# Last down products ahead of a combination, two pairs' bias loaded ahead, output weights ahead of the last two modulation chunks

## The chip, the cores and the metric

The kernel runs on one core of one Trainium2 chip. The metric is the device time of one execution, in microseconds (us); lower is better. TensorE (PE) multiplies into PSUM, VectorE (DVE), ScalarE (ACT) and GpSimd (POOL) work on SBUF and PSUM, and SyncE (SP) issues nearly all DMA transfers, in the order in which its program lists them. An engine runs its instructions in program order and waits on semaphores where another engine's result is needed.

## The reference

256 tokens of width 1024 pass through two blocks of two layers each. Every layer is a mixer followed by a mixture of experts (MoE), all in float32. The change touches the MoE of all four layers and the mixers of the second block.

```python
for i in range(DEPTH):                      # second block, DEPTH = 2
    mod = (silu(c) @ w_ada[i] + b_ada[i]).reshape(b, 6, d)        # modulation: 6 vectors of 1024
    hm = rmsnorm(x, norm_mix[i]) * (1 + sc_m) + sh_m
    y = dilated_mixer(hm, ...) if i == 0 else forgetting_mixer(hm, ...)   # ends with  o @ w_out
    x = x + g_m * y
    hf = rmsnorm(x, norm_ffn[i]) * (1 + sc_f) + sh_f
    x = x + g_f * hierarchical_moe_2(hf, ...)                     # top-1 group, top-2 experts of 16

# dilated mixer, for each of 16 head slots and three dilation groups:
logits = einsum(q, k) + bias            # bias from a table, by distance and head
p = softmax(logits); out = p @ v        # the groups' outputs merged by their softmax denominators

# mixture of experts
hid = silu(t @ w_gate[e]) * (t @ w_up[e])
y = sum over e of (hid * gate[e]) @ w_down[e]
```

The first block's two MoE have 32 experts, the second block's 16.

## The kernel before

**The weight ring.** All large weights pass through one buffer of 24576 columns in SBUF (`ring`). The class `Stream` (lines 49 to 96) fixes at build time the list of chunks in the order of the list, the place of each in the ring, and how many earlier chunks must have been given back (`chunk_used`) before a chunk may be loaded (`need`). `issue` walks that list in order on SP's queue: a chunk whose place isn't free yet holds back all behind it. A chunk is 4096 columns (2 MB) for 512 columns of a projection, 6144 columns (3 MB) for a modulation chunk (768 of w_ada's columns), 2048 columns (1 MB) for a third of an expert: pieces 0 and 1 hold gate and up for the lower and the upper half of k, piece 2 holds down.

**Modulation chunks.** 16 chunks of w_ada are slipped in among other weights by `weight_amid`. DVE turns one into partial sums by `ada_part` (lines 402 to 409, eight operations), then PE sums over the partitions by `ada_sums` (36 products of one column for three chunks), and DVE copies the result and finishes it (`after`).

**Output projection of the second block's mixers**, `project_rows` (line 426), called for `a_w_out_2` and `b_w_out_2` with `ada=[1, 2]`. Two weight chunks c = 0, 1, each with two units (one for each half of the tokens), eight K steps of 512 columns each. The chunks stand in the ring as modulation 1, weights 0, modulation 2, modulation 3, weights 1. DVE: copy of the gate row to `grow`, modulation chunk 1, units 0 and 1 (two operations each, in `add_rows`: times gate, plus x), modulation chunks 2 and 3, then units 2 and 3. A modulation chunk is given back when DVE has finished it, a weight chunk when DVE reaches its second unit (`free_chunk`). By the places in the ring, weights 1 lie where modulation chunk 1 lies, so that they can be loaded only when DVE has given that one back.

**Dilated attention**, `dilated_attention` (line 1103), twice (two halves of the heads), four pairs i of heads each. The bias of a pair is six DMAs of 128 KB (2 heads times 3 groups, `bias_load`, line 2757), which gather rows of a table in HBM. Pair 0's are issued before the half's projection ends, behind a wait until the last q and k rows have been turned (`load_last` in `project_heads_split`). Pair 1's are the first thing SP issues in the attention. Pair 2's wait until pair 0's logits are made, pair 3's until pair 1's are. DVE adds bias to scores and takes the maximum (L1216), ACT takes the exponential (L1255), DVE scales (L1224), PE transposes (L1175), ACT copies (L1263), PE multiplies by the values (L1185), in the order written out in `dilated_attention`.

**Experts**, `moe` (line 1294). For expert e PE runs, in this order: `gate_up(e + 1, 0)` (L1528), `turn(e)` (L1539, a transposition of the hidden rows), `combine(e - 1)` (L1561), `gate_up(e + 1, 1)`, `down(e)` (L1550). DVE: `hidden(e)` (L1771), `low(e - 1)` (L1791), `take_turned(e)` (L1775), `slots(e + 1)`. ACT: silu (L1653), then `high(e - 1)` (L1644). `down(e)` needs take_turned(e); `high(e)` needs down(e), `low(e)` needs high(e), `combine(e)` needs low(e). In the last expert the two gate_up are absent.

## Time and profile before

| | |
|---|---|
| three runs | 1701.11, 1706.50, 1706.56 us (median 1706.5) |
| profiled execution | 1701.91 us, span 1700.2 us, 1.7 us around the span |
| PE / PE weight load busy | 1559.8 us (92%) / 984.6 us (58%) |
| DVE / ACT / POOL busy | 809.8 us (48%) / 506.4 us (30%) / 135.8 us (8%) |
| mean granted TensorE clock | 0.963 |
| DMA | 467.27 MB, mean 275 GB/s |

A share of busy time says which engine is used most, not what a stage waits for. For each stage the time line and the waits tell what came last. The granted clock is the share of TensorE's full 2.4 GHz; it stands at 1.00 or at 0.50 (1.2 GHz), and a figure between the two is a stretch in which it changed. In a row of the time line "[0.36 <-PE PS L1539]" means that the engine was idle for 0.36 us before the instruction, until PE's L1539 released it. Rows with a count xN merge N instructions; the second number is then their common stretch.

The stages that the change touches, by their first and last instructions in the time line: the four MoE end at about 441, 875, 1384 and 1692 us; the dilated attention runs at 995.7 to 1040.9 and 1155.6 to 1200.3 us; the output projections at 1200.6 to 1240.2 and 1508.0 to 1547.6 us.

### The profile page before, as it was taken

The page shows a single profiled execution, that of the slowest core. Times are in us where ns is not written, and L with a number is a line of the kernel's source. Part 1 is how long each engine was busy: PE and PEld are TensorE (multiplying, and loading weights), DVE is VectorE, ACT ScalarE, POOL GpSimd, SP SyncE. Part 2 cuts the span into 40 slices and gives each one's busy share as a digit, 9 for nine tenths or more (in the row PEclk, how much of TensorE's full clock was granted, in tenths as well). Part 3 has the DMA queues.
Part 4 walks back from the last instruction along what each step waited for, and adds up shares of the span by engine and source line. Part 5 has one row for each costly group of instructions (what it writes and reads, how often), then busy time and mean ns, then how long its engine had stood idle before and what let it go on. Part 6 is the DMA issues. An engine that isn't in the chain of part 4 may idle for free. (4 is left out here: it accounts for less than half of the span.)

```text
span 1700.2 us, 23212 instructions
## 1 busy us (share of the span) xinstructions
PE 1559.8 (92%) x8906; PEld 984.6 (58%) x8906; DVE 809.8 (48%) x1863; ACT 506.4 (30%) x1015; POOL 135.8 (8%) x158
## 2 busy tenths in 40 slices
PE   8999899998799999999979988997889969889997
PEld 4585555554375555555447766775475547646553
DVE  1755533332335444333346645664663346576333
ACT  3230211111126212111135645555131135631211
POOL 0000211000000021001010001000021010002110
PEclk9999999999899989999999989999989989998999
DMA  8977289999761366999995351244449973626794
GB/s 365 371 285 282 90 357 420 421 421 420 314 277 75 126 249 247 420 421 420 421 398 222 137 211 51 100 180 166 177 173 400 421 320 124 248 92 257 300 421 196
DMA packets 62109, 467.27 MB, mean 275 GB/s; under 512 B 7664, under 2 KB 15776, under 8 KB 17184
## 3 DMA queue, kind: packets, MB, share of 16 engines
q1 hardware_dynamic: 61984, 465.59, 67.5%
q8 instruction: 79, 1.29, 0.3%
q14 instruction: 46, 0.38, 0.1%
HBM read 462.81 MB, written 2.76 MB: 274 GB/s over the span
## 5 line engine op out<-in xcount | busy, mean ns | idle before, releaser
L1528 PE MATMUL PS<-ring,catT 128*64 128x256 f32 x3072 | 368.5, 383 | 16.2 <-DMA ring<-in_moe 8.9
L1528 PEld LDWEIGHTS PS<-ring,catT 128*64 128x64 f32 x3072 | 213.6, 137 | 186.9 <-issue 82.1
L783 PE MATMUL PS<-w_split,h_split 128*128 128x512 f32 x1152 | 276.2, 398 | 10.4 <-DVE w_split L868 10.4
L783 PEld LDWEIGHTS PS<-w_split,h_split 128*128 128x128 f32 x1152 | 214.8, 190 | 65.3 <-DVE w_split L868 17.1
L1550 PE MATMUL PS<-ring,hidden_cols 128*64 128x512 f32 x768 | 183.1, 598 | 0.0
L868 DVE TENSOR_TENSOR w_split<-ring,w_split 128x512 fp32r<-128x512 f32 x192 | 131.9, 708 | 77.0 <-ACT w_split L816 76.6
L1791 DVE SCALAR_TENSOR_TENSOR xn_split<-PS,slot_w,xn_split 128x512 fp32r<-128x512 f32 x96 | 72.1, 751 | 192.1 <-ACT xn_split L1644 192.1
L816 ACT CAST w_split<-ring 128x512 fp32r<-128x512 f32 x192 | 118.2, 620 | 114.2 <-PE PS L783 113.7
L1653 ACT ACTIVATE hidden_rows<-PS 128x128 f32<-128x128 f32 x96 | 26.6, 277 | 412.8 <-PE PS L1528 412.8
L1561 PE MATMUL PS<-xn_split,back 64*128 64x512 f32 x768 | 114.4, 416 | 13.6 <-DVE xn_split L1791 13.5
L1644 ACT ACTIVATE xn_split<-PS,slot_w 128x512 fp32r<-128x512 f32 x96 | 66.0, 687 | 156.7 <-PE PS L1550 156.7
L1412 POOL COPY catT<-xsT 128x576 f32 x96 | 64.1, 668 | 584.2 <-PE PS L1528 517.3
L476 PE MATMUL PS<-ring,catT 128*128 128x512 f32 x224 | 100.3, 609 | 8.3 <-DMA ring<-in_b_w_out 3.7
L1771 DVE TENSOR_TENSOR hidden_rows<-PS,hidden_rows 128x128 f32<-128x128 f32 x96 | 28.0, 292 | 157.2 <-ACT hidden_rows L1653 157.2
L407 DVE SCALAR_TENSOR_TENSOR ada_part<-ring,silu_c,ada_part 128x768 f32<-128x768 f32 x98 | 99.9, 1019 | 3.4
L1550 PEld LDWEIGHTS PS<-ring,hidden_cols 128*64 128x64 f32 x768 | 53.9, 137 | 71.5 <-issue 56.9
L1561 PEld LDWEIGHTS PS<-xn_split,back 64*128 64x128 f32 x768 | 65.5, 184 | 36.7 <-issue 18.8
L476 PEld LDWEIGHTS PS<-ring,catT 128*128 128x128 f32 x224 | 43.5, 196 | 63.1 <-issue 54.2
L1396 POOL TENSOR_SCALAR xsT<-x,stat 128x1024 f32<-128x1024 f32 x8 | 22.8, 2846 | 684.3 <-DVE stat L1702 684.0
L1783 DVE SCALAR_TENSOR_TENSOR back<-catT,picked 128x256 fp32r<-128x256 f32 x96 | 46.5, 485 | 57.1 <-PE PS L1561 56.8
L1618 ACT ACTIVATE xn_split<-x 128x1024 fp32r<-128x1024 f32 x8 | 8.5, 1058 | 170.2 <-PEq L447 119.9
L1775 DVE COPY hidden_cols<-PS 128x128 f32<-128x128 f32 x96 | 28.0, 292 | 48.9 <-PE PS L1539 48.7
(417 smaller groups left out, 1811.5 us busy)
## 6 DMA issues: line engine op xcount, KB each, us to landing
ring<-in_moe SPq DMA_DIRECT2D x288, 1024.0 KB, 14.6
ring<-in_w_ada SPq DMA_DIRECT2D x16, 3072.0 KB, 14.0
ring<-in_a_w_in SPq DMA_DIRECT2D x23, 2048.0 KB, 10.0
ring<-in_b_w_in SPq DMA_DIRECT2D x8, 2048.0 KB, 17.8
ring<-in_a_w_out SPq DMA_DIRECT2D x2, 3072.0 KB, 10.3
ring<-in_b_w_out SPq DMA_DIRECT2D x2, 3072.0 KB, 10.4
ring<-in_w_mem_kv SPq DMA_DIRECT2D x2, 2048.0 KB, 12.1
ring<-in_a_w_out SPq DMA_DIRECT2D x2, 2048.0 KB, 8.3
```

The source lines that it names most:

```text
L407: dlink(nc.vector.scalar_tensor_tensor(part, w[:, k, :], silu_c[:, k:k + 1], part, ALU.mult, ALU.add))
L476: last = nc.tensor.matmul(PS[:, i % 8, 0:n], srcT[:, j, t * P:(t + 1) * P], w[:, j, o:o + n], start=j == 0, stop=j == k - 1)
L783: last = nc.tensor.matmul(PS[:, 2 * (i % 2) + t, :], hs[:, hp, k, t * P:(t + 1) * P], wk[:, (KT * i + k) % splits, wp, :], start=k == 0 an ...
L816: nc.scalar.copy(wk[:, (KT * i + k) % splits, 0, :], w[:, k, :]).then_inc(w_high.sem, 1)
L868: nc.vector.tensor_tensor(wk[:, (KT * i + k) % splits, 1, :], w[:, k, :], wk[:, (KT * i + k) % splits, 0, :].bitcast(F32), ALU.subtract).t ...
L1412: nc.gpsimd.tensor_copy(xf[:, e % 2], xsT[:, :, bass.ds(start, WIN)]).then_inc(win_ready.sem, 1)
L1528: last = nc.tensor.matmul(PS[half * WIN:(half + 1) * WIN, 4 + e % 2, 0:2 * P].rearrange("p (g f) -> p g f", g=2), xf[:, e % 2, k, :], gate ...
L1550: last = nc.tensor.matmul(PS[c * WIN:(c + 1) * WIN, 6 + e % 2, :], hs[:, e % 2, f2, :], wd[:, f2, c * BANK:(c + 1) * BANK], start=f2 == 0, ...
L1561: last = nc.tensor.matmul(PS[:, 2 * t + c, :], back[c * WIN:(c + 1) * WIN, e % 2, t * P:(t + 1) * P], yk(e % 2, h)[c * WIN:(c + 1) * WIN], ...
L1644: nc.scalar.activation(yk(e % 2, 0), PS[:, 6 + e % 2, :], ACT.Copy, scale=slot_w[:, e % 2, :]).then_inc(y_high.sem, 1)
L1783: nc.vector.scalar_tensor_tensor(back[:, e % 2, :], ranks[:, 1, :], slot_of[:, e:e + 1], picked[:], ALU.is_equal, ALU.add).then_inc(back_r ...
L1791: nc.vector.scalar_tensor_tensor(yk(e % 2, 1), PS[:, 6 + e % 2, :], slot_w[:, e % 2, :], yk(e % 2, 0).bitcast(F32), ALU.mult, ALU.subtract ...
```

## The change

Three edits.

1. In the last expert, PE does `down(E - 1)` ahead of `combine(E - 2)`, and DVE does `take_turned(E - 1)` ahead of `low(E - 2)`. All other experts stay as they were.
2. Pair 1's bias is issued together with pair 0's, in `load_last`. It goes to `grow` and to columns 5 to 7 of `catT`, instead of `grow` and a tile of its own; pair 3 still uses `grow` and that tile. SP's program in the attention begins with pair 2.
3. In the two output projections the ring's order becomes modulation 1, weights 0, weights 1, modulation 2, modulation 3. DVE does modulation chunks 1 and 2 ahead of units 0 and 1, and chunk 3 ahead of units 2 and 3. Modulation chunks 2 and 3 are given back together, behind unit 3.

```diff
-        c_aout2 = weight_amid("a_w_out_2", 8, [512] * 2, [1, 2])
+        c_aout2 = weight_amid("a_w_out_2", 8, [512] * 2, [1, 0], 2)
-        c_bout2 = weight_amid("b_w_out_2", 8, [512] * 2, [1, 2])
+        c_bout2 = weight_amid("b_w_out_2", 8, [512] * 2, [1, 0], 2)
@@ project_rows
-                    stream.issue(nc, sp, first + len(widths) + sum(ada))
+                    stream.issue(nc, sp, first + len(widths) + n_ada)
@@ project_rows, vector
                             for _ in range(ada[c]):
                                 ada_part(dve, ada0 + done, part[:, done, :])
                                 done += 1
-                            if ada[c] and done == sum(ada):
+                            if ada_last:
+                                ada_part(dve, ada0 + done, part[:, done, :], False)
+                                done += 1
+                            if done == n_ada:
                                 nc.vector.sem_inc(part_ready.sem, 1)
...
+                    for _ in range(ada_last):
+                        nc.vector.sem_inc(chunk_used, 1)
@@ dilated_attention, sync
-                    for i in range(1, n):
-                        if i >= 2:
-
-                            sp.wait_ge(*logits_ready[1].at(2 * (i - 1)))
+                    for i in range(2, n):
+                        sp.wait_ge(*logits_ready[1].at(2 * (i - 1)))
                         for y in range(2):
-                            bias_load(2 * i + y, bias[i % 2][y], bias_loaded[i % 2].sem)
+                            bias_load(2 * i + y, bias[i][y], bias_loaded[i % 2].sem)
@@ moe, tensor
                             turn(e)
-                            if e:
+                            if e + 1 < E:
+                                if e:
+                                    combine(e - 1)
+                                gate_up(e + 1, 1)
+                                down(e)
+                            else:
+                                down(e)
                                 combine(e - 1)
-                            if e + 1 < E:
-                                gate_up(e + 1, 1)
-                            down(e)
@@ moe, vector
                             hidden(e)
-                            if e:
+                            if e + 1 == E:
+                                take_turned(e)
                                 low(e - 1)
-                            take_turned(e)
+                            else:
+                                if e:
+                                    low(e - 1)
+                                take_turned(e)
@@ dilated mixer
-                        bias = [[first_bias[:, 0], first_bias[:, 1]]]
+                        other_bias = grow[:, 0:3 * T].rearrange("p (s k) -> p s k", s=3)
+                        bias = [(first_bias[:, 0], first_bias[:, 1]), (other_bias, catT[:, 5:8, :])]
-                        def load_first_bias(sp):
-                            for y in range(2):
-                                bias_load(y, bias[0][y], sig("bias_loaded0").sem)
+                        def load_two_biases(sp):
+                            for i in range(2):
+                                for y in range(2):
+                                    bias_load(2 * i + y, bias[i][y], sig(f"bias_loaded{i}").sem)
-                        bias.append([grow[:, 0:3 * T].rearrange("p (s k) -> p s k", s=3), sbuf(s2, "bias", [P, 3, T])[:]])
+                        bias += [bias[0], (other_bias, sbuf(s2, "bias", [P, 3, T])[:])]
-            project_rows(catT, 8, c_aout2, [512] * 2, add_rows(grow[:]), ada=[1, 2], after=...)
+            project_rows(catT, 8, c_aout2, [512] * 2, add_rows(grow[:]), ada=[1, 0], ada_last=2, after=...)
```

## Rows read from the trace of the kernel before

**Rows 1.** Waits of the whole span: us in total, times, longest.
```profile
PE PS L1561 <- DVE xn_split L1791: 13.5, 8, 1.8
DVE logits L1216 <- DMA bias<-bias_dram: 7.2, 2, 4.5
PE PS L476 <- DMA ring<-in_b_w_out: 3.7, 1, 3.7
PE PS L476 <- DMA ring<-in_a_w_out: 3.6, 1, 3.6
```

**Rows 2.** Time line, end of the fourth MoE: start us, us, engine, line.
```profile
1678.84 0.33 PE L1539 MATMUL PS<-ident,hidden_rows 128*128 128x128 f32 x1
...
1679.20 0.29 DVE L1775 COPY hidden_cols<-PS 128x128 f32<-128x128 f32 x1 [0.36 <-PE PS L1539]
...
1683.81 0.33 PE L1539 MATMUL PS<-ident,hidden_rows 128*128 128x128 f32 x1
...
1685.69 1.20 PE L1561 MATMUL PS<-xn_split,back 64*128 64x512 f32 x8 [1.55 <-DVE xn_split L1791]
...
1686.82 1.94 PE L1550 MATMUL PS<-ring,hidden_cols 128*64 128x512 f32 x8
```

**Rows 3.** Time line, end of the first MoE, the last down products.
```profile
434.75 3.62 PE L1550 MATMUL PS<-ring,hidden_cols 128*64 128x512 f32 x8
```

**Rows 4.** Table by stretches: us, busy by engine, granted clock, DMA share, GB/s.
```profile
436.00:438.00 2.00, 2.00 (x6) 0.24 (x2) 0.00 (x0) 0.00 (x0) 0.00 (x0) 0.50 0.98 418
...
1166.00:1168.00 2.00, 0.00 (x0) 0.00 (x0) 1.96 (x7) 1.30 (x4) 0.00 (x0) 0.50 0.55 189
...
1181.00:1182.00 1.00, 1.00 (x7) 0.67 (x4) 0.42 (x2) 1.00 (x3) 0.00 (x0) 1.00 0.06 22
```

**Rows 5.** Time line, first output projection of the second block.
```profile
1202.52 13.90 PE L476 MATMUL PS<-ring,catT 128*128 128x512 f32 x32
...
1203.98 0.62 DVE L405 TENSOR_SCALAR ada_part<-ring,silu_c 128x768 f32<-128x768 f32 x1
...
1212.06 0.33 SPq L93 DMA_DIRECT2D ring<-in_a_w_out  x1
1212.12 0.70 DVE L1289 TENSOR_TENSOR PS<-PS,grow 128x512 f32<-128x512 f32 x1
...
1212.86 0.69 DVE L1290 TENSOR_TENSOR x<-x,PS 128x512 f32<-128x512 f32 x1
...
1220.00 15.64 PE L476 MATMUL PS<-ring,catT 128*128 128x512 f32 x32 [3.58 <-DMA ring<-in_a_w_out]
...
1235.47 4.08 PE L423 MATMUL PS<-ones_f,ada_part 128*128 128x1 f32 x36
```

**Rows 6.** DMA issues at 1115 to 1117 us: KB each, us to landing.
```profile
ring<-in_w_ada SPq DMA_DIRECT2D x1, 3072.0 KB, 10.0
```

**Rows 7.** Time line, dilated attention of the first half.
```profile
1006.60 1.54 PE L1175 MATMUL PS<-ident,logits 128*128 128x128 f32 x6 [4.75 <-DVE logits L1224]
...
1014.03 2.01 PE L1185 MATMUL PS<-probsT,dv 128*64 128x128 f32 x24
```

**Rows 8.** Time line, dilated attention of the second half.
```profile
1165.92 0.56 DVE L1216 CUSTOM_DVE_ANT_1 logits<-PS,grow 128x384 f32<-128x384 f32 x1 [4.52 <-DMA bias<-bias_dram]
...
1168.29 1.54 PE L1175 MATMUL PS<-ident,logits 128*128 128x128 f32 x6 [6.57 <-DVE logits L1224]
...
1174.05 1.48 PE L1185 MATMUL PS<-probsT,dv 128*64 128x128 f32 x24
...
1174.45 1.81 SPq L2757 DMA_DIRECT2D grow<-bias_dram  x3
...
1178.92 0.88 PE L1175 MATMUL PS<-ident,logits 128*128 128x128 f32 x6 [0.66 <-DVE logits L1224]
...
1182.92 1.48 PE L1185 MATMUL PS<-probsT,dv 128*64 128x128 f32 x24
```

**Rows 9.** Time line, the third MoE's first expert products.
```profile
1273.51 5.40 PE L1528 MATMUL PS<-ring,catT 128*64 128x256 f32 x48 [1.87 <-POOL catT L1412]
```

More of the change, by code:

```diff
@@ L170, in build, with weight_amid @@
         ada_at = []
-        def weight_amid(name, k, widths, ada):
+        def weight_amid(name, k, widths, ada, ada_last=0):
             first = len(stream.chunks)
-            for ap, n in zip(chunk_aps(A[name], k, widths), ada):
+            for ap, n in zip(chunk_aps(A[name], k, widths) + [None], ada + [ada_last]):
                 for _ in range(n):
@@ L178, in weight_amid @@
                     stream.add([ada_aps[len(ada_at) - 1]])
-                stream.add([ap])
+                if ap is not None:
+                    stream.add([ap])
             return first
@@ L424, in ada_sums, with project_rows @@
             return last
-        def project_rows(srcT, k, first, widths, evac, cut=BANK, ada=None, after=None, aside=None, router=None, gate=None):
+        def project_rows(srcT, k, first, widths, evac, cut=BANK, ada=None, after=None, aside=None, router=None, gate=None, ada_last=0):
             ctx_rows = ExitStack()
@@ L433, in project_rows @@
             ada0 = sum(at < first for at in ada_at)
-            part = sbuf(ctx_rows, "ada_part", [P, sum(ada), 768]) if sum(ada) else None
+            n_ada = sum(ada) + ada_last
+            part = sbuf(ctx_rows, "ada_part", [P, n_ada, 768]) if n_ada else None
             part_ready, ada_made = sig("ada_part_ready"), sig("ada_made")
@@ L482, in _ @@
                             pe.wait_ge(*rows_taken.at(len(units)))
-                        ada_sums(sum(ada), part).then_inc(ada_made.sem, 1)
+                        ada_sums(n_ada, part).then_inc(ada_made.sem, 1)
                 def free_chunk(eng, i):
@@ L1214, in add_bias @@
                     def add_bias(i, t, y):
-                        nc.vector.tensor_tensor_reduce(logits(i, t, y), score(t, y), bias[i % 2][y][:, :, T - (t + 1) * P:T],
+                        nc.vector.tensor_tensor_reduce(logits(i, t, y), score(t, y), bias[i][y][:, :, T - (t + 1) * P:T],
                                                        1.0, 3.0e38, ALU.add, ALU.min, mx[:, i % 2, t, 0, y:y + 1]).then_inc(logits_ready[t].sem, 1)
@@ L2757, in bias_load @@
                                 nc.sync.dma_start(dst[:, g, :], src).then_inc(loaded, 16)
-                        def load_first_bias(sp):
-                            for y in range(2):
-                                bias_load(y, bias[0][y], sig("bias_loaded0").sem)
-                        project_heads_split(hT, c_ain2 + half * 9, jobs, rows=z_rows, load_last=load_first_bias,
+                        def load_two_biases(sp):
+                            for i in range(2):
+                                for y in range(2):
+                                    bias_load(2 * i + y, bias[i][y], sig(f"bias_loaded{i}").sem)
+                        project_heads_split(hT, c_ain2 + half * 9, jobs, rows=z_rows, load_last=load_two_biases,
                                             norm=(mod_gain[:, 0, 0, :], mod[:, 0, 0:8]) if half == 0 else None)
-                        bias.append([grow[:, 0:3 * T].rearrange("p (s k) -> p s k", s=3), sbuf(s2, "bias", [P, 3, T])[:]])
+                        bias += [bias[0], (other_bias, sbuf(s2, "bias", [P, 3, T])[:])]
                         def head(h):
@@ L2771, in build @@
                         dilated_attention([head(h) for h in range(8)], bias, bias_load)
-            project_rows(catT, 8, c_aout2, [512] * 2, add_rows(grow[:]), ada=[1, 2], after=lambda: modulation(1, (0, 24), (0,)), router=2, gate=mod[:, 0, 16:24])
+            project_rows(catT, 8, c_aout2, [512] * 2, add_rows(grow[:]), ada=[1, 0], ada_last=2, after=lambda: modulation(1, (0, 24), (0,)), router=2, gate=mod[:, 0, 16:24])
         if stop >= 7:
@@ L2843, in build @@
                 attention([head(h) for h in range(16)], True, key_bias, key_loaded)
-            project_rows(catT, 8, c_bout2, [512] * 2, add_rows(grow[:]), ada=[1, 2], after=lambda: modulation(1, (24, 48), (1,)), router=3, gate=mod[:, 1, 16:24])
+            project_rows(catT, 8, c_bout2, [512] * 2, add_rows(grow[:]), ada=[1, 0], ada_last=2, after=lambda: modulation(1, (24, 48), (1,)), router=3, gate=mod[:, 1, 16:24])
         if stop >= 9:
```

## The prediction

> **What bounds the kernel now.** I read the waits of the whole span first, because the shares of busy time say little here: PE is busy 92% of the span, so a gain must be a place where PE stands still, or runs at half clock, and nothing else covers it. Three kinds of such places answer to the three edits [rows 1]: PE waits for DVE ahead of a combination, 8 times and 13.5 us in all, two in each MoE's end; DVE waits for a bias load, twice, 7.2 us; PE waits for output weights, twice, 3.6 and 3.7 us. Then the time line around each place, to see what comes next if the wait goes. Last the granted clock there: it stands at 0.50 in the stretch behind each of the longer standstills [rows 4], so a removed wait can give back more than its own length.
>
> **Edit 1, the ends of the four MoE.** At the fourth, the last transposition starts at 1683.81, PE then waits 1.55 us for DVE's `low(14)`, combines at 1685.69 and starts the last down products at 1686.82 [rows 2]. In an ordinary expert DVE's copy of the transposed tile starts 0.36 us behind the transposition (1678.84, 1679.20) and takes 0.29 [rows 2]. With the copy first, it runs at 1684.17 to 1684.46, and down starts some 0.15 later, at 1684.6: 2.2 us earlier. DVE's `low(14)` isn't delayed: it ended just ahead of the combination at 1685.69, so it began about 1684.8, behind the copy. The moved combination (1.2 us) then runs between 1686.5 and 1687.7, while ACT and DVE turn the down products into `high` and `low`, in which time PE had nothing; the last combination only has to follow `low(15)`. All that comes later hangs on this chain, so 2.2 us come off. Bounds: 0 if the combination cost on the path what the reordering gives, 3.2 if both of PE's waits (1.55 and 1.8) went but for two latencies; I take 2.2. The other three ends have the same order. Four times 2.2 is **8.8 us**. The first MoE has a surplus: its last down products took 3.62 us instead of 1.94 [rows 2, 3], at a granted clock of 0.50 [rows 4]. Started 2.2 us earlier, at 432.6, they would be over by 434.5, ahead of where they now start; I count the difference, **1.7 us**, with 0 as the other bound. No wait is added: `low(E-2)` waits for ACT as before, and the copy ahead of it needs only the transposition.
>
> **Edit 2, the bias of pair 1.** Second half: DVE waited 4.52 us, until 1165.92 [rows 8]. Without the DMA, next is the scores of pair 1: PE had finished them when it went idle, at 1168.29 - 6.57 = 1161.72 [rows 8]. So DVE starts at about 1161.8, 4.1 us earlier, and PE's transposition follows it by 1168.29 - 1165.92 = 2.37 us, at 1164.2. First half: PE idle since 1006.60 - 4.75 = 1001.85, so its transposition can start at 1001.85 + 0.1 + 2.37 = 1004.3 instead of 1006.6 [rows 7]: 2.3 us. That is 6.4 us of plain waiting.
>
> Behind the wait comes the clock. From this transposition to the end of the value products the second half took 1174.05 + 1.48 - 1168.29 = 7.24 us, the first 1014.03 + 2.01 - 1006.60 = 9.44, and a later pair at full clock 1182.92 + 1.48 - 1178.92 = 5.48 [rows 7, 8]. The clock was 0.50 at 1166 to 1168 [rows 4]. If it stays up this gives back 1.8 and 4.0 us, 5.8 in all. The two bounds are 0 and 5.8. PE would still be idle for about 2.4 us, against 0.66 in a later pair [rows 8] and at most 1.8 in the MoE's ends [rows 1], of which the fourth kept the clock (1.94 us for down [rows 2]). I take 5.8. Sum of the edit: **12.2 us**.
>
> The six moved DMAs cost SP 3.7 us of issue (1.81 for three [rows 8], twice) in the projection, and what is behind them in the queue comes 3.7 us later: in the first half weights for the second half, in the second half the output weights and modulation chunks, wanted 50 us on. I cost that at nothing; it costs at most those 3.7 us if that cover is gone. Pair 2's bias still waits for pair 0's logits. It would be issued from about 1161.4; a quiet load of six went out at 1174.45 and its traffic ended by 1181 to 1182 [rows 4, 8], 7 us at most, so it lands by 1168.5. Pair 2 wants it about 1 us behind pair 0's values, 1169.6 + 1 = 1170.6. The slack is 2 us; in the first half 1001.5 + 7 = 1008.5 against 1010.8.
>
> **Edit 3, the output projections.** Now weights 1 are issued when modulation chunk 1 is given back (1212.06) and PE stands from 1216.42 to 1220.00; its second half then takes 15.64 us instead of 13.90 [rows 5]. With weights 1 early PE would be done at 1216.42 + 13.90 = 1230.3. Now DVE is the bound: three chunks of 8.05 us (1203.98 to 1212.06, less a little) and two units of 1.46 (0.70 and 0.69 with gaps) from 1203.98 make 1203.98 + 24.2 + 2.9 = 1231.1 [rows 5]. The 36 small products start at 1231.3 instead of 1235.47: **4.2 us**. What follows them is unchanged. Chunk 3 takes the wait that weights 1 had: issued at 1212.06, a 3 MB load on a quiet queue lands 10.0 us later [rows 6], 1222.1, and DVE wants it at 1223.0. It is hidden by 0.9 us. At best 5.3 us, if DVE had no part in it (3.58 and 1.74); the other way, each us that the load takes beyond 10.9 takes one off, and at 15.1 nothing is left. The other projection repeats the pattern [rows 1]. Twice 4.2 is **8.4 us**.
>
> The give-back moves: weights 0 from about 1216.5 to 1221.5, and the rest of the ring behind unit 3, at 1234. Ten of the next MoE's first twelve pieces (1 MB each) go out at 1232 to 1234. At 418 GB/s [rows 4] ten take 25 us, until 1259; PE wants the first at 1273.51 - 4.2 = 1269.3 [rows 9]. Hidden, by 10 us.
>
> One rule weighs on the clock term. PE's new idle stretch in the attention is a wait for DVE; at the first MoE's end PE had only waited for DVE (1.55 us and more) and was at 0.50 at 436 to 438 [rows 4]. The Trainium skill ("TensorE: Matmul & The Clock Gate", section "Loop structure matters more than you think") says that a DVE copy between groups of products leaves the array warm and that a wait for a DMA is what cools it. By it the 5.8 us are sure; by the row they are not, which is rival 1.
>
> **Sum.** 8.8 + 1.7 + 12.2 + 8.4 = 31.1 us. The profiled execution took 1701.91, so 1670.8. It lies at the lower of two levels of the runs (1701.1; 1706.5 twice), the median 4.6 above it. I know no term that says which level the changed kernel will take, and put the forecast in the middle: 1670.8 + 2.3 = **1673 us**.
>
> **Rivals.**
> 1. *The clock stays low.* PE is idle in the attention for 2.4 us and the small transpositions after it may run at 0.50 all the same, and so may the first MoE's last down. Against it: the later pairs and the fourth MoE's end kept it. Then 5.8 + 1.7 are missing: 1678.3 on the lower level, 1683 on the upper.
> 2. *The next load is late.* Chunk 3 lands 3 us later than I say, and pair 2's bias 1 us behind its need: twice 2.1 and twice 1, with 2 us of clock each time, 10 us: 1683. For it: slacks of 0.9 and 2 us. Against it: both queues are quiet then.
> 3. *The edits don't do what they say.* The bias still comes from behind something on SP's queue, or the moved combination lands on the path again (1.2 us of the 2.2 in each MoE, 4.8), and the attention gives nothing: 1701.9 - 31.1 + 12.2 + 4.8 + 2.3 = 1690.
> 4. *Slower: the experts' first weights come late.* Place: the third and the fourth MoE, since ten pieces are now issued only at 1232 to 1234. Price: each us by which they land behind 1269.3. It decides when both stand for over 15.5 us (31.1 in all), when ten pieces take over 51 us, a rate under 206 GB/s. While bias rows were gathered the rate was 189 GB/s [rows 4]; at it they take 55.5 us, landing at 1289, 20 us late, twice 40 us: 1702 + 9 = 1711. Against it: pieces of the ring moved at 418 [rows 4].
>
> **How the numbers follow.** Forecast 0.66, rival 1 0.19, rival 2 0.06, rival 3 0.03, slower 0.02, and 0.04 for a time below 1666 (more clock given back in the routers). The range takes in both levels and rivals 1 and 2: 1670.8 less 4 for terms that reach their better bound, 1667, to 1684. What measurement can tell from no change is about 0.3%, 5 us: faster 0.96, same 0.02, slower 0.02.
>
> **What would show it.** Right: no idle time of DVE before L1216 for a bias DMA, PE's transposition about 2.4 us after it fell idle, clock 1.00 there; L476 as one run of 64 products in 27.8 us, then under 1 us before the small products; DVE's L1775 ahead of L1791 at the MoE's ends, with 2.4 us from the transposition's end to PE's next combination. Wrong: a clock of 0.50 behind either attention's first pair; a wait of DVE for w_ada or of L1216 for z_rows; any wait of L1528 for the ring at the third MoE's start.

## The result and the profile after

The changed kernel took 1689.0 us (median of four runs, 1676.21 to 1689.67), the kernel before, run beside it, 1706.5; the ratio is 0.9881, with a 95% interval of 0.9836 to 0.9927. Six more runs of it later gave 1688.4 (1678.60 to 1692.52; 0.989, 0.9854 to 0.9927). So it is faster by 1.2%, about 19 us, where 31 us and 1673 were forecast. The profiled execution took 1689.67 us, with a span of 1687.9 and a mean granted clock of 0.955, against 1701.91, 1700.2 and 0.963 before.

Every wait that the prediction set out to remove is gone or as small as forecast. What comes behind them isn't as forecast: the granted clock, and two waits of PE that grew.

The waits of the whole span, after (engine, line waited for, us in total, times, longest). They answer to [rows 1]: 8 waits of 13.5 us ahead of a combination are 4 of 2.7 us, and there is no row of L1221 (L1216 before) waiting for a bias DMA, nor of L478 (L476 before) waiting for the ring.

```profile
PE PS L1566 <- DVE xn_split L1799: 2.7, 4, 0.7
PE PS L424 <- DVEq L525: 1.6, 2, 0.8
```

The time line at the end of the fourth MoE, PE alone (start us, us). It answers to [rows 2].

```profile
1673.69 0.33 PE L1544 MATMUL PS<-ident,hidden_rows 128*128 128x128 f32 x1
1674.45 1.94 PE L1555 MATMUL PS<-ring,hidden_cols 128*64 128x512 f32 x8 [0.43 <-issue]
1676.32 1.20 PE L1566 MATMUL PS<-xn_split,back 64*128 64x512 f32 x8
1678.20 1.20 PE L1566 MATMUL PS<-xn_split,back 64*128 64x512 f32 x8 [0.67 <-DVE xn_split L1799]
```

From the last transposition to the last down products it is 0.76 us (forecast: 0.79), and the moved combination stands in a time in which PE had nothing.

The time line of the second half's attention, DVE's first operation on pair 1 and PE behind it. It answers to [rows 8].

```profile
1150.53 0.55 DVE L1221 CUSTOM_DVE_ANT_1 logits<-PS,grow 128x384 f32<-128x384 f32 x1
...
1153.16 1.54 PE L1180 MATMUL PS<-ident,logits 128*128 128x128 f32 x6 [2.24 <-DVE logits L1229]
1154.63 1.23 PE L1147 MATMUL PS<-dkT,dqT 64*128 64x256 f32 x4
1155.79 1.54 PE L1180 MATMUL PS<-ident,logits 128*128 128x128 f32 x6
```

DVE has no idle time ahead of it, and PE waits 2.24 us (forecast: 2.4). But both transpositions take 1.54 us, the time of half clock, where a later pair takes 0.88 [rows 8]. The table by stretches says the same (us, busy by engine with the number of instructions, granted clock, DMA share, GB/s):

```profile
1153.00:1157.00 4.00, 3.84 (x16) 2.79 (x16) 1.99 (x6) 1.90 (x6) 0.00 (x0) 0.50 0.49 167
```

The time line of the first output projection and the start of the router behind it, PE alone. It answers to [rows 5].

```profile
1190.33 27.63 PE L478 MATMUL PS<-ring,catT 128*128 128x512 f32 x64
1218.75 5.62 PE L424 MATMUL PS<-ones_f,ada_part 128*128 128x1 f32 x36 [0.79 <-DVEq L525]
1226.25 3.64 PE L1436 MATMUL PS<-ident,x 128*128 128x128 f32 x16 [1.89 <-PEq L449]
1229.69 3.44 PE L1442 MATMUL PS<-catT,mod 128*128 128x20 f32 x16
1232.96 6.99 PE L1448 MATMUL PS<-catT,hT 128*128 128x20 f32 x32
```

The projection is one run of 64 products, as forecast. Then the small products take 5.62 us instead of 4.08 [rows 5], since the clock falls 2.4 us behind their start, PE stands for 1.89 us, and the router's products run at half clock. The kernel before, in the same place:

```profile
1240.49 3.55 PE L1431 MATMUL PS<-ident,x 128*128 128x128 f32 x16 [0.94 <-PEq L447]
1243.87 1.86 PE L1437 MATMUL PS<-catT,mod 128*128 128x20 f32 x16
1245.58 5.50 PE L1443 MATMUL PS<-catT,hT 128*128 128x20 f32 x32
```

The stretch of after, by the table by stretches: PE is busy for 14.75 of 15 us, and the clock doesn't come back.

```profile
1226.00:1241.00 15.00, 14.75 (x70) 14.79 (x71) 3.90 (x11) 4.69 (x7) 9.94 (x4) 0.50 1.01 421
```

The wait of 1.89 us (0.94 before) ends just behind SP's last issue of the experts' weights, most of which edit 3 holds back until unit 3. SP's row in the same stretch is over at 1225.81, 0.44 us ahead of PE's 1226.25:

```profile
1219.58 6.23 SPq L93 DMA_DIRECT2D ring<-in_moe  x10
```

Behind the third MoE, PE's first transpositions of the next mixer wait for PE's own sequencer, and longer than before. Before, after, and in the kernel with zeros in the attention and around the small products (f_both, described below):

```profile
1394.04 3.58 PE L769 MATMUL PS<-ident,catT 128*128 128x128 f32 x16 [9.59 <-PEq L1301]
1384.50 3.65 PE L776 MATMUL PS<-ident,catT 128*128 128x128 f32 x16 [12.22 <-PEq L1306]
1371.02 3.65 PE L780 MATMUL PS<-ident,catT 128*128 128x128 f32 x16 [8.73 <-PEq L1313]
```

### The profile page after: what moved, and what is told of

The parts are those of the page before. It is cut to its first block and busy times, and to the rows that moved or that the text cites. A ratio compares the mean times of both kernels' runs of the same rounds, so it can differ in the third digit from the quotient of the medians.

```text
span 1687.9 us, 23214 instructions
## 1 busy us (share of the span) xinstructions
PE 1569.2 (93%) x8906; PEld 994.5 (59%) x8906; DVE 807.0 (48%) x1863; ACT 506.3 (30%) x1015; POOL 136.4 (8%) x158
## 5 line engine op out<-in xcount | busy, mean ns | idle before, releaser
L478 PE MATMUL PS<-ring,catT 128*128 128x512 f32 x224 | 96.7, 592 | 1.1 <-PEq L982 1.1
L478 PEld LDWEIGHTS PS<-ring,catT 128*128 128x128 f32 x224 | 42.3, 190 | 53.3 <-issue 53.3
## 6 DMA issues: line engine op xcount, KB each, us to landing
ring<-in_moe SPq DMA_DIRECT2D x288, 1024.0 KB, 14.9
ring<-in_w_ada SPq DMA_DIRECT2D x16, 3072.0 KB, 12.2
ring<-in_b_w_in SPq DMA_DIRECT2D x8, 2048.0 KB, 17.6
ring<-in_b_w_out SPq DMA_DIRECT2D x2, 3072.0 KB, 10.5
```

The lines of the kernel that those rows point to most:

```text
L478: last = nc.tensor.matmul(PS[:, i % 8, 0:n], srcT[:, j, t * P:(t + 1) * P], w[:, j, o:o + n], start=j == 0, stop=j == k - 1)
```

## The experiments

Two things were open. First, whether each edit is worth what was forecast, alone and beside the others. Second, whether the lowered clock is what took the rest, and what lowers it. Unless a line says otherwise a time is the median; "alone" is the kernel before with one edit. All were timed against the kernel before on the same chip, and ratios come with their 95% intervals. In the profile rows, tiles named `PS<-zero` are products of zeros; `keep_busy(bank, n)` issues n of them, 512 columns each. The kernel before has some of its own, in the routers.

### Each edit alone

The edits are those of the diff above, one at a time; the extracts below only name them.

**Edit 1 alone.**

```diff
 moe: last expert
-combine(e - 1); down(e)        low(e - 1); take_turned(e)
+down(e); combine(e - 1)        take_turned(e); low(e - 1)
```

> The kernel before with edit 1 alone (the order in the last expert of each MoE). Theory (the waits went as forecast, TensorE's clock took part of it back): the four ends give 8.8 us and the first MoE's last down nothing more, since the clock falls just behind it: about 6 to 9 us off. Rival (the prediction's terms hold, each edit by itself): 8.8 + 1.7 = 10.5 us off.

Measured: 1699.16 us (12 runs), ratio 0.9954 (0.9934 to 0.9975), 7.2 us under the kernel before. The theory, though the interval (4.3 to 11.3 us) holds the rival's 10.5 too.

**Edit 2 alone.**

```diff
-load_last=load_first_bias
+load_last=load_two_biases
```

> The kernel before with edit 2 alone (pair 1's bias loaded with pair 0's). Theory: both waits for a bias DMA are gone, 6.4 to 8 us, but the granted clock is 0.50 behind the first pair as before, for 7 to 10 us, so that the transposition that took 1.54 us still takes 1.54: 5 to 8 us off in all. Rival: the clock stays at 1.00 there, the transposition takes 0.88 us, 12.2 us off.

Measured: 1693.48 us (8 runs), ratio 0.9936 (0.9905 to 0.9967), 12.9 us by the medians. By this run alone it is the rival. Its profile shows the waits gone, and a granted clock that did fall in the attention: in the first half the transposition took 1.54 us again (in the second half 0.88, and the one behind it 1.54).

```profile
1001.71 1.54 PE L1173 MATMUL PS<-ident,logits 128*128 128x128 f32 x6 [2.24 <-DVE logits L1222]
1003.18 1.23 PE L1140 MATMUL PS<-dkT,dqT 64*128 64x256 f32 x4
```

**Edit 3 alone.**

```diff
-ada=[1, 2]
+ada=[1, 0], ada_last=2
```

> The kernel before with edit 3 alone (the order of weights and modulation chunks in the two output projections). Theory: the projection is one run of 64 products in some 27.7 us and the small products start 4 us sooner, but they and the router behind them then stand at a granted clock of 0.50 for 20 us or more where it was 10, which costs 4 to 5 us each: between 1 us faster and 3 us slower in all. Rival: 8.4 us off, the clock has no part in it.

Measured: 1698.32 us (12 runs), ratio 0.9958 (0.9937 to 0.9980), 8.0 us by the medians. Neither theory's loss nor a proof of the rival: the router behind the first projection took 1.7 us more than before, and PE's wait for SP at its start was 2.60 us instead of 0.94, which is nearly all of it; the other router lost nothing.

**The changed kernel again.**

> The changed kernel again, to see how far its times lie apart. Theory: the time follows the share of the span at half clock, so that runs with a mean granted clock near 0.967 are near 1676 us and those near 0.956 near 1689 us, and nothing lies below the line through them. Rival: the two levels have to do with the DMA, and the mean clock of a run says nothing about its time.

Measured: 1688.43 us (6 runs). The time does follow the clock: the run at 1678.60 has a mean granted clock of 0.964, that at 1692.52 has 0.953. But the line isn't sharp, and it isn't a matter of this kernel: the 68 runs of the kernel before that were made beside the experiments lie anywhere from 1694.0 to 1713.8 us (median 1705.5, mean 1704.9), its mean clock from 0.954 to 0.964. Five runs at 0.963 or more have a mean of 1698.7 us, thirteen at 0.956 or less one of 1708.7.

By their medians the three edits alone add up to 28 us, and together they gained 18. With such a scatter that can be chance, so kernels with one edit left out were run as well.

### One edit left out

```diff
 no_rows:  edits 1 and 2      no_bias:  edits 1 and 3      no_tails:  edits 2 and 3
```

> The changed kernel without edit 3 (edits 1 and 2 alone). By the single edits' medians, 7.2 and 12.9 us off, it stands at 1686 us. Theory (edit 3's wait is gone in the changed kernel, but its routers run at half clock and give it all back): 1684 to 1689 us, no slower than the changed kernel's 1688.7. Rival (edit 3 is worth its 4.2 us for each projection in the changed kernel too, and what is missing is missing elsewhere): 1695 to 1697 us.

Measured: 1689.76 us (6 runs), ratio 0.9916 (0.9892 to 0.9940).

> The changed kernel without edit 2 (edits 1 and 3). By the single edits, 7.2 and 8.0 us off: 1691 us. Theory (edit 2 is worth its two waits, 6.4 to 8 us, and no clock): 1695 to 1697 us. Rival (edit 2 is worth 12 us as forecast): 1701 us.

Measured: 1695.22 us (12 runs), ratio 0.9940 (0.9921 to 0.9960).

> The changed kernel without edit 1 (edits 2 and 3). By the single edits, 12.9 and 8.0 us off: 1685 us. Theory (edit 1 is worth 7 to 9 us on its own chain, at each MoE's end): 1696 to 1698 us. Rival (what is missing in the changed kernel is missing at the MoE's ends): 1688 to 1691 us.

Measured: 1691.18 us (12 runs), ratio 0.9935 (0.9913 to 0.9958).

Without edit 3 the time is 0.8 us above its theory's range, without edit 2 it is in its theory's (1695 to 1697), without edit 1 it is at its rival's (1688 to 1691). With intervals 7 to 8 us wide none decides by itself. Taken together they do. I fitted one time to each edit over all 140 runs of the kernels that hold any mix of the three (68 of before, 72 of the others), which assumes that the edits add up:

| edit | forecast | measured by the fit | measured in the segments below |
|---|---|---|---|
| 1, MoE ends | 10.5 | 5.7 ± 0.8 | 6.8 |
| 2, bias | 12.2 | 8.7 ± 0.8 | 8.7 |
| 3, output projections | 8.4 | 4.3 ± 0.8 | 4.0 |
| sum | 31.1 | 18.8 ± 1.0 | 19.5 |

(± is one standard error.) The fit meets the mean of each of the eight mixes within 1 us. Terms for pairs of edits, put into it, come out at 0.1 to 1.5 ± 1.7 us: no sign that one edit eats another, though 3 us of it couldn't be told. The 28 us of the single edits can be scatter; by means they are 25.

The third column is a second way to the same numbers, from the traces. The same DVE instruction is looked up in nine profiles (before, the changed kernel twice, and the six mixes), and the time between two such instructions is compared, kernels with the edit against kernels without it (means in us, with the least and the greatest, and behind them the mean us at a granted clock of 0.50 in the segment):

| segment | without | with | difference |
|---|---|---|---|
| first MoE's end, to 30 us behind it | 38.9 (37.6 to 40.4), 10.2 | 37.0 (35.9 to 37.4), 12.3 | -1.9 |
| second | 43.6 (43.3 to 43.8), 8.5 | 42.0 (41.2 to 42.5), 9.5 | -1.6 |
| third, to the next projection | 135.3 (134.8 to 135.6), 19.6 | 134.1 (133.1 to 134.9), 19.8 | -1.2 |
| fourth, to the kernel's end | 17.6 (17.4 to 17.8), 6.4 | 15.4 (15.3 to 15.4), 6.3 | -2.2 |
| attention, first half, start to pair 0's output | 19.6 (19.2 to 20.1), 11.1 | 16.8 (15.9 to 17.2), 9.5 | -2.8 |
| second half | 21.1 (18.8 to 22.1), 12.0 | 15.2 (14.2 to 17.4), 5.4 | -5.9 |
| output projection 1, to the small products' copy | 38.1 (36.7 to 39.5), 6.2 | 34.0 (33.9 to 34.1), 3.5 | -4.1 |
| router behind it, to the first expert | 38.1 (38.0 to 38.1), 10.8 | 41.1 (39.8 to 43.3), 18.4 | +3.1 |
| output projection 2 | 38.3 (36.8 to 39.6), 6.3 | 34.0 (32.4 to 35.0), 2.8 | -4.4 |
| router behind it | 38.0 (37.7 to 38.1), 10.7 | 39.4 (38.0 to 43.2), 14.9 | +1.4 |

The fourth MoE's end, where the time at 0.50 is the same with and without the edit, gives its 2.2 us within 0.4 in every kernel. Most of the scatter is in segments where the time at 0.50 scatters too: the same code of the second attention took 18.82 us with 6.8 us at 0.50 in the kernel before, and 21.99 with 13.7 in the kernel with edit 1 alone.

Three parts of these segments aren't the clock, and the table hides them:

- From the last expert's `hidden` to DVE's first operation on the residual rows it is 9.28 us without edit 1 and 7.03 with it, at all four ends and in all nine profiles but for one value: 10.97 at the first end of the kernel before. So edit 1's chain gives its 2.25 us at every end.
- Behind the third MoE, PE stood for 9.6 to 10.3 us without edit 1 and 11.8 to 12.7 with it, and the trace names PE's own sequencer. The other engines' rows of the same line of the program stand 1.0 to 1.7 us ahead of PE's start without edit 1 and 3.2 to 4.1 us with it. From the last `hidden` to the mixer's first DVE operation on `hT` the means are 23.9 us without and 23.8 with: nothing is left of edit 1 there, and the 1.2 us in the table come from further on. In the seven kernels with zeros below that have none at the MoE's ends this wait is 8.7 us, also where the zeros stand far from it. What holds PE's sequencer isn't shown.
- At the first router's start PE waited 0.94 us without edit 3 and 1.30 to 2.63 with it, a mean of 2.05; at the second's 1.63 in the changed kernel and 0.94 in the other eight profiles (0.30 where zeros stand ahead of it). In all nine routers of all kernels, with zeros or without, in which this wait was longer than usual, PE began 0.44 or 0.45 us behind the end of SP's last issue of expert weights; in the others SP had been done earlier. So 1.2 of the 4.5 us that the routers lost are SP's issues. That is read from the distance; no run issues them at another time.

### Holding the clock up

If a pause or light work of PE lowers the clock, products of zeros in its place must hold it. They write a part of PSUM that nobody reads.

**Zeros in the attention**, in the changed kernel:

```diff
                         if j == 2:
+                            if i == 0:
+                                for _ in range(18):
+                                    nc.tensor.matmul(PS[:, 3, 2 * P:4 * P], zero[:, 0:P], zero[:, 0:2 * P], ...)
                             pe.wait_ge(*probs_ready[1].at(i + 1))
```

> The changed kernel plus 18 products of zeros (256 columns, bf16, results never read) where PE waits 2.24 us for DVE ahead of the third transposition of pair 0, in both attentions. Theory (PE's pause there is what lowers the clock, and the lowered clock is what ate edit 2's second term): the stretch from the attention's start to pair 0's output falls from 14.2 to 17.4 us to about 14 us in both halves, no 0.50 there, some 5 us off in all against the changed kernel. Rival (the clock falls for what PE did before the pause, or the stretch is bound by DVE and ACT): the pause is filled, the stretch keeps its 16 to 17 us and its slow clock, no change.

Measured: 1672.98 us (5 runs), ratio 0.9817 (0.9794 to 0.9839), 15 us under the changed kernel, three times the theory's 5. The time line of PE and then the table by stretches, first half:

```profile
997.52 2.14 PE L1178 MATMUL PS<-zero 128*128 128x256 bf16 x18
999.83 0.87 PE L1183 MATMUL PS<-ident,logits 128*128 128x128 f32 x6 [0.17 <-DVE logits L1232]
```

```profile
998.00:1002.00 4.00, 3.83 (x32) 2.82 (x29) 3.11 (x9) 3.34 (x11) 0.00 (x0) 1.00 0.41 117
```

The clock is 1.00, the transposition takes 0.87 us, and from the attention's start to pair 0's output it is 12.7 us in both halves, against 17.0 and 17.4. That is 9.0 us. The rest isn't in the attention: between the two profiles 3.0 us more are gone in the first projection with its router, 4.2 behind the third MoE and 4.3 in the second projection with its router, in code that this edit doesn't touch. Of the 4.2, 3.5 are PE's wait for its own sequencer (8.72 us instead of 12.22), not the clock. How much of the rest the edit brings about, and how much is where the clock happened to stand in either profile, is left open.

**Zeros around the small products**:

```diff
+                        keep_busy(5, 3)
                         pe.wait_ge(*part_ready.at(1))
                         ada_sums(n_ada, part).then_inc(ada_made.sem, 1)
+                        keep_busy(5, 4)
```

> The changed kernel plus products of zeros around the 36 small products of both output projections, three (512 columns, bf16) ahead of them, where PE waits 0.8 us, and four behind them, where it waits 1.3 to 1.9 us. Theory one (the idle time around the small products starts the slow stretch): the stretch from the projection's end to the router's gather returns from 24.4 us to 21 us, 3 us off for each. Theory two (the small products of one column themselves count as little work): the clock still falls in them, nothing gained, up to 0.5 us lost each.

Measured: 1677.58 us (5 runs), ratio 0.9833 (0.9808 to 0.9859). Theory one's stretch: 20.3 and 20.2 us from the projection's output to the gather, instead of 24.6 and 24.4. In both the clock still fell in the small products, which took 5.6 and 5.7 us, as theory two had it, but it was back soon after the zeros. The time is 11 us under the changed kernel; the routers give 6.0 of them against the mean of the kernels with edit 3, and PE's wait behind the third MoE 3.5 against the profile of the changed kernel.

```profile
1219.16 5.62 PE L424 MATMUL PS<-ones_f,ada_part 128*128 128x1 f32 x36
1224.65 1.87 PE L354 MATMUL PS<-zero 128*128 128x512 bf16 x4
1226.81 2.73 PE L1440 MATMUL PS<-ident,x 128*128 128x128 f32 x16 [0.30 <-PEq L449]
1229.38 1.86 PE L1446 MATMUL PS<-catT,mod 128*128 128x20 f32 x16
```

So here the loss is less in how it begins than in that it doesn't end.

**And among the small products**, two for every three:

```diff
                     for m in range(6):
+                        if m % 3 == 0:
+                            keep_busy(5, 2)
```

> As the kernel with zeros around the small products, and 12 more products of zeros among the 36 small ones, two for every three. They cost 12 x 0.21 = 2.6 us at full clock in each projection. Theory two (the small products are what lets the clock fall): small products and fillers run at clock 1.00, some 6.7 us instead of 5.7, and the router behind them at 1.00, which gives 3 to 5 us back, so 1 to 3 us off in each. Theory one (only the idle time counts): 2.6 us lost in each against the kernel without them.

Measured: 1676.37 us (5 runs), ratio 0.9822 (0.9798 to 0.9846). The clock is 1.00 in the small products now, the mechanism of theory two, but neither number came: not 1 to 3 us off in each, nor 2.6 lost. By the profiles projection and router together are 0.5 us longer than without these zeros, both times; the two times can't be told apart.

**Both, attention and around the small products.**

> The changed kernel with the zeros in the attention and those around the small products together. Theory: both gains add, 8 to 11 us off against the changed kernel, near 1678 us. Rival (what one slow stretch gives up another takes, since the slow stretches only move): no more than the better of the two alone.

Measured: 1672.20 us (5 runs, 1668.06 to 1673.09), ratio 0.9801 (0.9779 to 0.9824): 0.8 us better than the attention alone, which is within the scatter. The rival. The profile says where it went. In the first projection the small products ran at full clock (4.18 us), the clock fell behind them at 1216.0, and four zeros at half clock didn't bring it back:

```profile
1211.71 4.18 PE L424 MATMUL PS<-ones_f,ada_part 128*128 128x1 f32 x36
1215.75 1.63 PE L354 MATMUL PS<-zero 128*128 128x512 bf16 x4
1218.17 3.65 PE L1443 MATMUL PS<-ident,x 128*128 128x128 f32 x16 [0.79 <-PEq L449]
1221.61 3.44 PE L1449 MATMUL PS<-catT,mod 128*128 128x20 f32 x16
```

And further on in the same router, by the table by stretches:

```profile
1226.00:1231.00 5.00, 5.00 (x25) 5.00 (x25) 0.00 (x0) 0.00 (x0) 4.83 (x2) 0.50 1.01 421
```

**All three, attention, around and among the small products.**

> The changed kernel with the zeros in the attention, around the small products and among them. Theory (the slow stretch that begins in or just behind the small products is started by PE's light work there, and the zeros among them keep the first router at 20.2 us from output to gather instead of 24.7): 2.6 us paid and 4.5 won in the first projection, 2.6 paid and 1.8 won in the second, 1671 us. Rival (it moves to the router and begins there): 1675 us.

Measured: 1668.92 us (5 runs, 1662.78 to 1671.67), ratio 0.9784 (0.9762 to 0.9805). As the theory had it, and the fastest kernel of the study: 1.2% under the changed kernel, 2.2% under the one before. The router in it, in the same place, by the time line of PE and then by the table by stretches:

```profile
1218.36 1.94 PE L1445 MATMUL PS<-ident,x 128*128 128x128 f32 x16 [0.30 <-PEq L451]
1220.13 1.86 PE L1451 MATMUL PS<-catT,mod 128*128 128x20 f32 x16
1221.84 3.73 PE L1457 MATMUL PS<-catT,hT 128*128 128x20 f32 x32
```

```profile
1216.00:1224.00 8.00, 7.70 (x66) 6.85 (x65) 3.33 (x10) 4.69 (x7) 2.25 (x1) 1.00 1.01 426
```

### The edits with the clock held

**The kernel before with zeros** in the attention, in the wait for weights 1 and around the small products. In words, its zeros are:

- 42 products of zeros (256 columns) ahead of pair 0's third transposition
- `keep_busy(5, 15)` ahead of the wait for weights 1
- `keep_busy(5, 3)` ahead of the small products, `keep_busy(5, 4)` behind them

> The kernel before with products of zeros in the same places as the kernel with both sets of zeros (attention and small products), more of them where its waits are longer: 42 for the wait for the bias, 15 for the wait for weights 1. Theory (the waits of the three edits are worth 8.8 + 6.4 + 8.4 = 23.6 us whatever the clock does, and the clock is a term of its own): 1672 + 24 = 1696 us, some 10 us below the kernel before. Rival (what the zeros gave was in truth the edits', or the edits' terms were wrong in size): under 1688 or over 1702 us.

Measured: 1693.46 us (6 runs), ratio 0.9929 (0.9913 to 0.9946). The kernel with the edits and these zeros took 1672.20: the edits are worth 21.3 us here, forecast 23.6 for their waits (each of the two times is uncertain by 3 to 4 us). The attention's segments are 16.4 and 16.9 us against 12.7 twice, so edit 2's waits are 7.9 us. There was no 0.50 in either attention of this kernel, though PE still paused for 1.21 and 1.75 us behind the zeros. Its second use is as a test of the projection's old order with the wait for weights 1 filled: the clock stood at 1.00 through both projections' weights, and the routers then had 18.2 and 13.7 us at 0.50, where the four kernels of the old order without zeros had 10.2 to 11.6. Its time line shows DVE's two waits for the bias, 3.84 and 4.38 us:

```profile
1005.58 0.56 DVE L1225 CUSTOM_DVE_ANT_1 logits<-PS,grow 128x384 f32<-128x384 f32 x1 [3.84 <-DMA bias<-bias_dram]
...
1161.48 0.56 DVE L1225 CUSTOM_DVE_ANT_1 logits<-PS,grow 128x384 f32<-128x384 f32 x1 [4.38 <-DMA bias<-bias_dram]
```

**All zeros, without edit 3.**

> The kernel with zeros in the attention, around and among the small products (1669 us), without edit 3, and with 15 zeros more while PE waits for weights 1. Theory (with the clock held, edit 3 is worth its forecast 4.2 us for each projection): 1677 us. Rival (edit 3 is worth nothing even then, the projection's end being set by something else): 1669 to 1671 us.

Measured: 1676.04 us (6 runs), ratio 0.9832 (0.9806 to 0.9858), against 1668.92: edit 3 is worth 7.1 us when the clock is held, as the theory had it (8.4). By the times alone that isn't clear of the 4.3 us without zeros; the profiles say where it lies. The projections take 37.9 and 38.4 us without edit 3 and 34.5 twice with it, 7.3 us together, and of the routers behind them the first takes the same (35.9 and 35.8), the second 0.7 us less with it.

### Zeros at the MoE's ends too

```diff
                         nc.tensor.sem_inc(y_ready.sem, 1)
+                        if m < 3:
+                            keep_busy(7, (30, 28, 37)[m])
```

> The kernel with both sets of zeros, and products of zeros behind the last combination of the first three MoE too, where PE waits 6.6 to 8.7 us for the residual rows and the norm. Theory (the 10 to 14 us at 0.50 behind each MoE's end come from that wait, and edit 1 never touched them): they go, the transpositions behind take 1.9 instead of 3.65 us, 2 to 4 us off for each MoE, 1662 to 1666 us. Rival: the stretch behind is bound by DVE and ACT, no change at 1672 us.

Measured: 1675.61 us (5 runs), ratio 0.9841 (0.9816 to 0.9866), slower than without them (1672.20). At the first MoE's end they did what they should: 36.3 us, none at 0.50, instead of 37.4. At the second the segment took 48.9 us instead of 41.1, since PE's transpositions broke off for 4.24 us, for no cause that the trace names. The forecast of 2 to 4 us off for each MoE was missed.

```profile
865.68 5.77 PE L354 MATMUL PS<-zero 128*128 128x512 bf16 x26
874.36 1.09 PE L780 MATMUL PS<-ident,catT 128*128 128x128 f32 x4 [2.90 <-PEq L1313]
879.68 2.72 PE L780 MATMUL PS<-ident,catT 128*128 128x128 f32 x12 [4.24 <-issue]
```

**All of it, and four in the third and fourth MoE's routers.**

> All these zeros together (attention, around and among the small products, MoE ends) and four more among the router's products of 20 columns in the third and fourth MoE. Theory: no long slow stretch is left but at the picks, a mean granted clock over 0.975, 1660 to 1664 us. Rival (the zeros now cost what they give): 1668 us or more.

Measured: 1677.43 us (5 runs), ratio 0.9840 (0.9818 to 0.9861), with the highest mean clock of all, 0.980. The rival. The second MoE's end is 47.3 us here, with a stop of PE of 4.50 us in the same place. What stops it stays open.

## Why the prediction was wrong

**The base held.** The forecast stood on 1704.2 us for the kernel before (the profiled 1701.91 and 2.3). The mean of 68 runs is 1704.9. The reason given for it, two levels, was wrong: it is a wide scatter, 1694 to 1714, that goes with the clock.

**Edit 1: 8.8 + 1.7 forecast, 5.7 to 6.8 measured.** The wait's term is right at all four ends: 2.25 us on the chain in every profile, 9.0 in all against 8.8, and the time line at the fourth end is the one forecast. The failed step is "All that comes later hangs on this chain, so 2.2 us come off", taken four times. It holds at the fourth end, where the kernel is over. Behind the first and the second some 0.8 and 0.7 us were lost again, in stretches with 2.9 and 1.8 us more at 0.50. Behind the third all of it was: PE's wait for its own sequencer grew by 2.1 us, a wait that the prediction didn't have at all; further on 1.0 us came back where the clock scatters. Why PE starts later there stays open. The 1.7 us of the first MoE's last down products were a draw: in the execution that I read they fell into a stretch at 0.50 [rows 3, 4], and the chain took 10.97 us; in the three other kernels with the old order it took 9.3.

**Edit 2: 6.4 + 5.8 forecast, 8.7 measured.** The waits were worth more than I said, 7.9 us: the execution that I read had the shortest of them, DVE's two waits for the bias being 2.70 and 4.52 us there, 7.2 in all, and 7.3 to 8.2 in the four other profiles without the edit. The step that failed is the clock: "If it stays up this gives back 1.8 and 4.0 us", of which I took all 5.8. It gave 0.8 (8.7 less 7.9). A pause of 2.24 us, in which PE waits for DVE and for no DMA, was followed by 0.50 in both halves of all five profiles with edit 2, in eight of the ten at the next transposition and in two at the one behind it. Rival 1 had this as its mechanism and 0.19 as its chance; the evidence taken against it, the later pairs (pause of 0.66 us) and the fourth MoE's end (at most 1.8 us), was of shorter pauses, and the evidence for it was in the rows: the first MoE's end. That the pause is the cause is shown by the zeros: with them in its place the clock was 1.00 in both halves of each of the seven kernels that had them. The Trainium skill ("TensorE: Matmul & The Clock Gate", section "Loop structure matters more than you think") has a DVE copy between groups of products leave the array warm, with the next products following immediately. Here they follow 2.24 us later, and the clock fell in ten cases of ten, so "By it the 5.8 us are sure" read more into that sentence than these traces bear out.

**Edit 3: 8.4 forecast, 4.3 measured.** The term itself is right: 4.1 and 4.4 us in the segments, one run of 64 products, 0.79 us ahead of the small products, no wait for chunk 3, which landed 0.6 us ahead of its use (0.9 forecast). The failed sentence is "What follows them is unchanged": the routers lost 3.1 and 1.4 us. Of these, 1.2 us are the give-back. The prediction asked only when the experts' pieces land, and was right there; it left out that the router can't begin until SP has issued them, which in the changed kernel made PE's wait at the first router 1.89 us instead of 0.94. The other 3.3 us go with the clock. In both orders it falls in the small products or just behind them: in them in four of eight cases with the old order, in nine of ten with the new. With the old order it is back after 3.4 or 6.8 us, falls once more in the router's light work, and the router has 10.2 to 11.6 us at 0.50. With the new order it stays down for up to 24 us, with PE busy nearly all the time, and the router has 10.6 to 24.1. Two experiments speak for the clock as the cause of this part: with zeros around and among the small products the router has 3.4 to 10.2 us at 0.50 in all eight cases, and edit 3 is worth 7.1 us. Zeros around them alone are no such proof: they left it at 6.8 to 20.5. That the pause for weights 1 protected the router behind it isn't shown; for it speaks the kernel of the old order with this pause filled (18.2 and 13.7 us), which had other zeros too. A pause put back into the changed kernel wasn't run.

**In sum.** By the segments, against the forecast's steps: 25.4 us of waits (9.0, 7.9 and 8.5) where 23.6 were forecast (21.3 measured by the times with zeros in both kernels); 1.2 us of clock to be won (0.8, and 0.4 for the first MoE's down products in one profile of four) where 7.5 were; and 7.1 us lost behind the edits where nothing was (4.5 in the routers; 2.6 behind the first three MoE, the 1.0 us that came back already taken off). That is 19.5 us, and 18.8 by the fit. Rival 1's own time, 1678 to 1683, was still too low, because it priced the clock in the attention and in the first MoE's down products alone. Rivals 2 and 3 play no part: no transfer was late, and the edits did what they say. Nor does rival 4: the first two of the experts' pieces went out at 1208.8 and 1209.1, the other ten at 1219.6 to 1225.4, the last landed at 1248.1, and PE's first product on them began at 1261.9, behind POOL as before. What edit 3's give-back cost was SP's time to issue them, not their landing.

## What to carry to other kernels

When a wait of TensorE is taken away, its price and its clock are two terms: read the wait's worth from the time line, and give the clock no credit unless PE's remaining pause is as short as one behind which the trace shows 1.00. Look at what runs next: here the dense products of a projection had the clock back after 3.4 or 6.8 us, a router's light ones were at 0.50 for up to 24, and so a wait removed ahead of light work cost later part of what it saved. Look also at who else has to be done before the next stage: issues of DMAs that are put off can end up as its last condition. Products of zeros in a pause that can't be closed went with as large a gain as the whole change here (20 us of 1689, of which some 3 are PE's own late start behind the third MoE, which went away with them for no reason known), but they have to be placed one by one and measured; at the MoE's ends they cost more than they gave.

One profiled execution is one draw: segments with the same code differed by up to 5.2 us between profiles (the second router with edit 3, 38.0 to 43.2), so a clock term read from one trace should be looked for in a second.

## What the runs showed that I had not expected

- The granted clock stayed at 0.50 while PE was busy 14.75 of 15 us with transpositions and products of 20 columns; being busy didn't bring it back.
- The same 36 small products took 4.08 to 4.18 us at full clock and 5.62 with 3.1 us of it at 0.50, that is, half of the time at 0.50 was lost; the router's 32 products of 20 columns took 3.73 and 6.99.
- PE began a stage up to 4 us behind the other engines, with its own sequencer named as the cause, and this wait was 0.9 to 4.0 us shorter in kernels that differ from the others in products of zeros elsewhere.
- The mean granted clock of a run explains most of the scatter of this kernel: over 68 runs of the kernel before the correlation with the time is -0.82, some 1.3 us for each 0.001.
